# Two k groups of the MLP down products as seven block products in place of eight

## The reference

```python
def sq_relu_mlp(x, w_up, w_down):          # x 256 x 1024, w_up 1024 x 4096, w_down 4096 x 1024
    h = jax.nn.relu(x @ w_up)
    return (h * h) @ w_down

h = h + rms_norm(sq_relu_mlp(rms_norm(h, mpre), w_up, w_down), mpost)   # after each of two mixers
```

## Time and profile before

| | us |
|---|---|
| median of 3 runs (1108.02 to 1108.41) | 1108.19 |
| span of the profiled execution, first to last instruction | 1106.3 |
| PE busy | 1098.5 |
| DVE busy | 806.6 |
| ACT busy | 636.1 |
| POOL busy | 150.0 |

### The profile page before, as it was taken

One profiled execution on the slowest core, in us unless ns is written; L12 is line 12 of the kernel. 1 busy time (PEld: TensorE's weight loads), 2 busy tenths in 40 slices (PEclk: granted clock), 3 DMA queues, 4 the chain that ended last, 5 costly groups with the idle time before them and its releaser, 6 DMA issues.

```text
span 1106.3 us, 13497 instructions
## 1 busy us (share of the span) xinstructions
PE 1098.5 (99%) x5131; PEld 913.3 (83%) x5131; DVE 806.6 (73%) x920; ACT 636.1 (58%) x787; POOL 150.0 (14%) x111
## 2 busy tenths in 40 slices
PE   9999999999999999999999999999999999999997
PEld 7788888888888888888888888888888888888886
DVE  5785768776678873778448569998467976899942
ACT  7656576655767653654587366654355655756431
POOL 1434600000344310000023000000005000000000
PEclk9999999999999999999999999999999999999999
DMA  9645444555455555655435446546555334654530
GB/s 355 247 172 183 144 161 162 200 190 190 186 195 190 190 195 185 229 200 197 183 115 195 166 179 258 188 156 229 193 188 208 122 145 171 225 174 180 191 145 38
DMA packets 30503, 205.16 MB, mean 185 GB/s; under 512 B 3624, under 2 KB 3792, under 8 KB 6768
## 3 DMA queue, kind: packets, MB, share of 16 engines
q1 hardware_dynamic: 28752, 198.75, 49.4%
q0 software_dynamic: 1696, 5.64, 1.6%
HBM read 203.33 MB, written 1.05 MB: 185 GB/s over the span
## 4 chain that ended last, share of the span: by engine, by line
PE 96%; DVE 2%; ACT 1%; issue 0%; DVEq 0%; ACTq 0%
PE ps L685 84%; PE ps L1139 3%; PE aux L757 3%; PE ps L1141 1%; PE ps L800 1%; PE aux L1006 1%; PE aux L1176 1%; PE aux L991 1%; PE ps L877 0%; PE aux L1163 0%; PE ps L793 0%; DVE Wl L1833 0%; ACT Wh L1303 0%; DVE prob L2050 0%; ACT bprob L1777 0%
## 5 line engine op out<-in xcount | busy, mean ns | idle before, releaser
L685 PE MATMUL ps<-Wh,xT 128*128 128x512 f32 x1792 | 560.1, 391 | 0.0
L1833 DVE TENSOR_TENSOR Wl<-raw,Wh 128x2048 fp32r<-128x2048 f32 x183 | 422.6, 2317 | 151.3 <-ACT Wh L1303 150.3
L1303 ACT ACTIVATE Wh<-raw 128x2048 fp32r<-128x2048 f32 x183 | 349.0, 1914 | 187.6 <-PE ps L685 187.5
L685 PEld LDWEIGHTS ps<-Wh,xT 128*128 128x128 f32 x1792 | 336.4, 188 | 69.9 <-issue 0.3
L685 PE MATMUL ps<-Wl,xT 128*128 128x512 f32 x896 | 348.6, 389 | 0.0
L685 PEld LDWEIGHTS ps<-Wl,xT 128*128 128x128 f32 x896 | 168.3, 188 | 34.1
L685 PE MATMUL ps<-Wh,hTh 128*128 128x512 f32 x256 | 99.7, 389 | 0.0
L685 PE MATMUL ps<-Wh,hTl 128*128 128x512 f32 x256 | 99.6, 389 | 0.0
L685 PE MATMUL ps<-Wl,hTh 128*128 128x512 f32 x256 | 99.6, 389 | 0.0
L2392 DVE STREAM_TRANSPOSE htmp<-held 32x512 f32<-32x512 f32 x128 | 90.0, 703 | 2.7
L637 POOL TENSOR_TENSOR sc<-sc,cst 128x1 f32<-128x1 f32 x8 | 4.5, 559 | 443.6 <-DVE sc L2352 443.6
(11 more groups left out here) (355 smaller groups left out, 1310.6 us busy)
## 6 DMA issues: line engine op xcount, KB each, us to landing
raw<-in_wstream SPq DMA_DIRECT2D x185, 1024.0 KB, 4.8
grow<-in_post_gains POOLq DMA_DIRECT2D x4, 512.0 KB, 6.2
grow<-in_b_gate POOLq DMA_DIRECT2D x6, 256.0 KB, 3.4
mrows<-in_mem SPq DMA_DIRECT2D x2, 512.0 KB, 5.3
raw<-in_wstream SPq DMA_DIRECT2D x2, 512.0 KB, 6.5
x<-in_x SPq DMA_DIRECT2D x1, 1024.0 KB, 13.5
out<-x SPq DMA_DIRECT2D x4, 256.0 KB, 2.0
rdm<-in_ret_decays POOLq DMA_DIRECT2D x1, 768.0 KB, 5.1
```

The source lines that it names most:

```text
L685: mm = nc.tensor.matmul(ps[2 * pair + t][:, :], a[:, kt, t * P:(t + 1) * P], w[:, slot, j, :], start=(first and j == 0 and q == 0), stop=( ...
L1303: nc.scalar.activation(split_view(Wh, g), weight_view(raw, g), ACT.Copy).then_inc(hi_ready, 1)
L1833: nc.vector.tensor_tensor(split_view(Wl, g), weight_view(raw, g), split_view(Wh, g).bitcast(F32), ALU.subtract).then_inc(lo_ready, 1)
```

## The change

In each MLP the first two k groups (512 rows of k each) of both down units are no longer multiplied block by block. With the two tiles of tokens, the two k groups and the two halves of the columns they are a 2 x 2 by 2 x 2 product of blocks, done by Strassen's scheme (in Winograd's form) with seven block products Q1 to Q7 in place of eight. A block product is 12 matmuls. All k groups from 2 on stay as they were.

The mixed rows (sums of blocks of h) are made on DVE in `mix_rows`, after `low_pair(0)`, then cut into high and low parts in the place of `xT`. The sums of weight blocks are made by the loads: a slot of `raw` that still holds one block is loaded again with `accum_op=ALU.add`, from POOL's queue. So the granules of both units come in 13 positions for `down_0` (seven Q and the groups 2 to 7) and six for `down_1`, 19 where there were 16. Every position is loaded and split. Block sums are made in PSUM: ACT copies Q1 and Q6 with a minus sign into other banks, PE adds onto them, Q5, Q3 and Q7 are taken out to SBUF, and DVE adds them up in `add_parts` and once after Q4. The order of positions is `FAST_ORDER`.

SP's loop over the weight loads is written out, and some semaphores of the head norms in the first block become one with counts (not shown).

```diff
+FAST_ORDER = ["Q1", 2, 3, 4, "Q5", 5, "Q3", 6, "Q6", "Q2", "Q7", 7, "Q4"]
+FAST_LOAD = {"Q1": (0, 0, False), "Q5": (1, 0, True), "Q6": (1, 1, True), "Q4": (0, 1, True),
+             "Q3": (1, 1, False), "Q7": (1, 0, True), "Q2": (0, 1, False)}
...
# POOL, after after_mix("p2", ...) and after after_mix("p4", ...)
+                for g in range(P0[name], P1[name]):
+                    if ADDED[g]:
+                        pool.wait_ge(lo_ready, g + 1 - RING)
+                        pool.dma_start(raw[:, g % RING, :, :], wstream[SRC[g]], accum_op=ALU.add)\
+                            .then_inc(added[CHAIN[g]], 16)
...
# PE
+            def fast_product(m, rows_ready_for):
+                mixed = {"Q5": 0, "Q6": 1, "Q7": 2, "Q3": 3}
+                plain = {"Q1": (0, 0), "Q2": (1, 0), "Q4": (1, 1)}
+                for k, what in enumerate(FAST_ORDER):
+                    g = P0[n0] + k
+                    if what in FAST_LOAD:
+                        if what == "Q1":
+                            rows_ready_for(0)()
+                            bank_read(n0)(0)
+                            o = bank(n0, 0)
+                        elif what == "Q5":
+                            pe.wait_ge(sem("mix_low"), m + 1)
+                            o = open_aux(f"fast{m}", 0)[:, :]
...
+                        elif what == "Q6":
+                            o = bank(n1, 0)
+                        elif what == "Q2":
+                            rows_ready_for(1)()
+                            o = bank(n0, 0)
+                        elif what == "Q7":
+                            pe.wait_ge(sem("fast_copy"), 3 * m + 2)
+                            o = bank(n1, 1)
...
+                        pe.wait_ge(lo_ready, g + 1)
...
+                    for t in (1, 0) if k == 1 else (0, 1):
+                        if k == 1:
+                            if t == 1:
+                                bank_read(n0)(1)
+                            else:
+                                pe.wait_ge(sem("fast_copy"), 3 * m + 1)
+                        mm = half_granule(...)
...
+                pe.wait_ge(sem("fast_sum"), 2 * m + 1)
...
# ACT, behind the loop: for n in range(8): up(n); high_pair if n >= 3 and odd; squared_rows(n)
+                for k in range(len(FAST_ORDER) - 1):
+                    if k == AT["Q1"]:
+                        fast_copy("Q1", bank(n1, 0), bank(n0, 0), -1.0)
+                    elif k == AT["Q6"]:
+                        fast_copy("Q6", bank(n1, 1), bank(n1, 0), -1.0)
+                    elif k == AT["Q7"]:
+                        fast_copy("Q7", partz[:, :], bank(n1, 1), 1.0)
+                    elif k == AT["Q5"]:
+                        fast_part("Q5", 0, part5)
+                    elif k == AT["Q3"]:
+                        fast_part("Q3", 1, part3)
+                    elif k == 3:
+                        high_pair(3)
+                    split(P0[n0] + k + RING)
+                    if k == 0:
+                        act.wait_ge(sem("mix_rows"), m + 1)
+                        act.wait_ge(gran_used, P0[n0])
+                        nc.scalar.activation(mixh[:, :, :, :], mixr[:, :, :, :], ACT.Copy).then_inc(sem("mix_high"), 1)
...
# DVE
+                def mix_rows():
+                    a11, a12 = htmp[:, 0:4, 0:P], htmp[:, 4:8, 0:P]
+                    a21, a22 = htmp[:, 0:4, P:TOK], htmp[:, 4:8, P:TOK]
+                    link(nc.vector.tensor_tensor(mixr[:, 0, :, :], a21, a22, ALU.subtract))
+                    link(nc.vector.tensor_tensor(mixr[:, 1, :, :], a11, mixr[:, 0, :, :], ALU.subtract))
+                    nc.vector.tensor_tensor(mixr[:, 2, :, :], a11, a21, ALU.subtract)
+                    nc.vector.tensor_tensor(mixr[:, 3, :, :], a12, mixr[:, 1, :, :], ALU.subtract).then_inc(sem("mix_rows"), 1)
...
                     if late:
                         low_pair(k)
+                        if k == 0:
+                            mix_rows()
                         turn_pair(k + 1, 0, 4)
...
+                for k in range(len(FAST_ORDER) - 1):
+                    if k < 3:
+                        turn_pair(3, 4 * k + 4, 4 * k + 8)
+                    elif k == 3:
+                        low_pair(3)
+                    elif k == AT["Q7"]:
+                        add_parts()
+                    split(P0[n0] + k + RING)
+                    if k == 0:
+                        dve.wait_ge(sem("mix_high"), m + 1)
+                        nc.vector.tensor_tensor(mixl[:, :, :, :], mixr[:, :, :, :], mixh[:, :, :, :].bitcast(F32), ALU.subtract)\
+                            .then_inc(sem("mix_low"), 1)
+                wait_unit(dve, n0, 1)
+                nc.vector.tensor_tensor(bank(n0, 1), bank(n0, 1), partz[:, :], ALU.add).then_inc(sem("fast_sum"), 1)
+                gained(p, n0, 0, post_k)()
```

More of the change, by code:

```diff
@@ L431, in build @@
         landed = [sem(f"landed{i}") for i in range(RING)]
+        added = [sem(f"added{i}") for i in range(2)]
         hi_ready = sem("hi_ready")
@@ L500, in _ @@
             sp.dma_start(raw[:, 3, :, :], wstream[3]).then_inc(landed[3], 16)
[L501 to L508, removed]
+            for g in range(RING, NP):
+                if not ADDED[g]:
+                    sp.wait_ge(lo_ready, g + 1 - RING)
+                    sp.dma_start(raw[:, g % RING, :, :], wstream[SRC[g]]).then_inc(landed[g % RING], 16)
             for t in range(2):
@@ L708, in kts_of @@
             def kts_of(name, g):
-                k0 = sum(KTS[G[name]:g])
-                return range(k0, k0 + KTS[g])
+                return TILES[g]
             def product(name, operand, before=None, leave=0, bank_free=None):
                 th, tl = operand
[L715 to L718, removed]
+                for g in range(P0[name], P1[name] - leave):
+                    if before and g - P0[name] in before:
+                        before[g - P0[name]]()
+                    granule(g % RING, g + 1, th, tl, kts_of(name, g), U[name] % 2, g == P0[name], g == P1[name] - 1,
                             bank_free or bank_read(name))
@@ L1216, in rows_ready_for @@
                     return lambda: pe.wait_ge(sem("h_low"), 8 * m + q + 1)
-                product(f"down{m}_0", (hTh, hTl), before={q: rows_ready_for(q) for q in range(8)})
-                product(f"down{m}_1", (hTh, hTl), leave=RING)
+                fast_product(m, rows_ready_for)
+                for g in range(P0[f"down{m}_1"], P1[f"down{m}_1"] - RING):
+                    granule(g % RING, g + 1, hTh, hTl, TILES[g], U[f"down{m}_1"] % 2, False, False, None, True)
                 tile_by_tile(steps_of([f"down{m}_1"], (hTh, hTl)),
@@ L1305, in unit @@
             def unit(name, read_out=None, *urgent):
[L1308 removed]
+                for g in range(P0[name], P1[name] - 1):
                     split(g + RING)
@@ L1749, in mlp @@
+                down_squares(p, n0, 0, (0,))
+                act.wait_ge(sem("fast_sum"), 2 * m + 2)
+                down_squares(p, n0, 0, (1,))
+                split(P1[n0] - 1 + RING)
+                for g in range(P0[f"down{m}_1"], P1[f"down{m}_1"] - RING):
                     split(g + RING)
                 if after:
-                    cross(GEND[f"down{m}_1"], f"{after}T", gain, lambda t: down_squares(p, f"down{m}_1", 1, (t,)))
+                    cross(P1[f"down{m}_1"], f"{after}T", gain, lambda t: down_squares(p, f"down{m}_1", 1, (t,)))
@@ L2439, in mlp @@
                 if gain:
-                    cross(GEND[f"down{m}_1"], f"{after}T", gain, rows)
+                    cross(P1[f"down{m}_1"], f"{after}T", gain, rows)
                 else:
```

277 lines of the change are left out of this document (178 added, 99 removed).

## The result

The changed kernel took 1120.96 us (median of 4 runs, 1120.73 to 1121.06) against 1108.12 us for the kernel before, a ratio of 1.0114 with a 95% interval of 1.0102 to 1.0127. It is slower by 12.8 us; the forecast was 1118.0 us, 9.8 us slower, with a range of 1113 to 1125. The profiled execution took 1121.05 us, 1.85 us above its span.

A forecast was written before the change was run, and what follows sets the result against it. TensorE was taken as the bound, VectorE nearly a second one at the seam. Each MLP: 7.6 us of stalls less 2.7 us of saved matmuls, +4.9; both +9.8 on 1108.2 gives 1118.0 us, range 1113 to 1125.

The forecast's parts named there:

- The sign: Whole kernel: slower than before, chance 0.92; faster 0.05, within 0.2% of no change 0.03.
- the first stall: Position 1 of the first down unit: TensorE waits for ScalarE's copy of Q1, 5.65 us in each MLP.
- The second stall: Positions 5 and 7: TensorE waits for VectorE's splits, 1.6 us at position 7; all stalls then reach 7.6 us.
- rival 4: TensorE slow after the position 1 stall: 2.2 us lost, net +0.6 in each MLP, 1119.2 to 1123.6 us; chance 0.07.
- The accumulating loads: Weight-sum loads for Q5, Q6, Q7, Q4: 9.6 us each, bounds 4.8 to 13.5, costing nothing up to 11 us.
- rival 1: Added loads take over 11 us, tightest for Q7 and Q4: 1123 us at 13.5 us, about 1128 at 16; chance 0.20.
- the main term: TensorE's new wait at position 1 for ScalarE's copy of Q1: 5.65 us in each MLP.
- Rival 2: Not slower: Q1's copy is covered at position 1 and VectorE's additions fit, 1102.8 us; chance 0.06, 0.05 on 1102.8.

The follow-up runs named there:

- the last order: Changed kernel with its positions reordered, two second-unit groups among the products, three free banks for products, and VectorE's steps reordered: 1103.19 us, ratio 0.9952 to the kernel before.

## Why the prediction was right, and where its sum was short

- **The sign, and the first stall.** Forecast 5.65 us, ended by ScalarE's copy behind high_pair(2), itself waiting for VectorE; measured 5.55 us, each step of the queue within 0.1 us. mix_rows was put at 2.75 us; its rows run from 693.49 to 696.36 with the hand-over, 2.87.
- **The second stall.** Forecast 0.3 + 1.6 us at positions 5 and 7. The changed kernel shows neither; the run with PE kept busy shows the one at position 7, 1.28 us. It was there and covered by the half clock. The one at position 5 shows in the run with the copy moved up, 0.68 us.
- **The slow array, rival 4, came true** (0.07). Forecast 2.2 us of loss, net +0.6 in each MLP; measured 2.33 us (5.05 - 2.72) and 2.47 (5.19 - 2.72), in place of the second stall's 1.9: net 0.4 and 0.6. The run without it gained 0.4 us in both MLPs together. The nine slow matmuls that the rival took its price from ran at a granted clock of 1.00, so that the price came out nearly the same is luck. The Trainium skill ("TensorE: Matmul & The Clock Gate", section "HAM oscillation — how this bites in real kernels") has the lower clock level at half of the upper one, 1.2 for 2.4 GHz; the trace agrees: 1.00 ahead of the gap, 0.50 behind it.
- **The accumulating loads: the term that was mis-sized**, and rival 1 came true (0.20). I took 9.6 us for all and found 11.2 us of room for Q4's. Three of four took 7.9 to 8.2 us, Q4's 12.8 and 12.1. That is 1.6 and 0.9 us over; PE waited 1.1 and 0.5 us for the sum. The step that failed is the last of its argument, that 15% of the DMA engines are free and so sharing costs little. That was a mean over a stretch of 61 us; in the 15 us around Q4's load 2% are free. The plain load in the same place, with 6% free, took 4.9 us, so it is adding and sharing together that cost the time; how one makes the other dearer stays open. The room was 0.4 us larger than I found: the 8.2 us for the work behind the load should have been 8.8 by its own parts and took 8.4 (landing at 783.01, sum at 791.41), and PE came to the sum at 790.2, not 789.7. Beyond that room of 11.6 us each microsecond cost about one, as forecast. The estimate by the rule of the Trainium skill ("Collectives: The Full Stack", section "The bandwidth ceiling: the fold count and why AG ≠ RS ≠ AR") was 7.7 us for an added load; outside Q4's place 8.0 was measured, where the run with plain loads took 5.0.
- **Together** the slow array (0.4 and 0.6 us net), the first stall (0.1 us shorter in each MLP) and the sum (1.4 and 0.8 us with the 0.3 beside each wait) are 1.7 and 1.3 us, and 1118.0 + 3.0 = 1121.0. The range held both rivals at once.
- **What the prediction saw only in part.** It called the wait for the copy the main term. The runs say that the copy was hardly a cause: without it the time is the same, since VectorE ends the stretch at 768 us in any case. The prediction's own sum has this unsaid: its stalls of 7.6 us are 767.95 - 760.3, the end of VectorE's queue, whatever the copy does, so the number was right with the wrong wait in front. Rival 2, which let the time fall to 1102.8 if the copy was covered "and VectorE's additions fit", failed on its second condition: with the copy covered the time stayed at 1120.61. And VectorE's slack was named by the split of position 7 (it starts at 758.87, is ready at 761.2 and is wanted at 768.5); the narrow place is low_pair(3), whose first half is ready near 762.3 in the earlier trace rows where PE wants it at 730.40 + 6 x 5.44 = 763.0. These 0.7 us are the slack that the runs put at 0.84 by PE's idle time, and they cap the gain of any saving on PE ahead of that place.

## What to carry to other kernels

Before work is taken from a bound engine, ask how much slack the next engine has at each place where it hands over: here it was some 0.8 us, and a saving of 2.72 us in each MLP, without any cost, left the median where it was. Where a second engine is saturated for a stretch, cutting single waits of the first only moves them; put work in between that needs nothing from the late engine, and nearly the same work, with loads that took longer, turned from 1.1% slower to 0.5% faster. The largest row in the list of waits is the one that ends last at its place, not the one whose removal pays: move it in thought, and see what PE meets next.

## What the runs showed of the hardware that I had not expected

- Behind a gap of 5.4 us PE ran at half clock (0.50) for 4.8 us, in both MLPs; behind a gap of 3.25 us (the copy moved up) matmuls ran 0.43 us apart, too; behind a gap of 1.88 us they did so in one MLP (from 1045.46 on) and not in the other (762.94). Filling the gap with matmuls kept it at 1.00.
- A load of 1 MiB that adds to SBUF took 7.9 to 8.2 us in three places of the changed kernel and 12.8 and 12.1 in the fourth; the same loads without adding took 4.9 to 5.1, and 4.9 and 6.2 in the fourth. In the last order it took 8.0 to 13.6. Its issue kept POOL for 0.87 us, where the plain one took 0.53.
- A wait of PE cost some 0.3 us more than its idle time in the trace: 0.15 in the gap and 0.1 to 0.15 in the spacing of the matmuls behind it.
